# Forgetting attention: next head's first two units scored beside the last unit, with one score buffer that swaps sides per head

## The reference

```python
q = q.reshape(b, lp, B_HEADS, HEAD_DIM)          # 8 heads of 64; k and v alike
cum = jnp.swapaxes(jnp.cumsum(log_f, axis=1), 1, 2)
for i in range(lp // Q_BLOCK):                    # 128 queries at a time
    lo, hi = i * Q_BLOCK, (i + 1) * Q_BLOCK
    s = jnp.einsum('bqhd,bkhd->bhqk', q[:, lo:hi], k[:, :hi]) * (HEAD_DIM ** -0.5)
    s = s + cum[:, :, lo:hi, None] - cum[:, :, None, :hi]
    mask = (idx[None, :hi] <= idx[lo:hi, None]) & key_valid[None, :hi]
    p = jax.nn.softmax(jnp.where(mask, s, -jnp.inf), axis=-1)
    outs.append(jnp.einsum('bhqk,bkhd->bqhd', p, v[:, :hi]))
```

## Time and profile before

| what | us |
|---|---|
| median of the runs | 2371.5 |
| profiled execution, its own time | 2372.46 |
| span of its trace | 2370.8 |
| forgetting attention, from first to last transposes | about 503 (648 to 1151) |
| TensorE busy, whole span | 2140.1 (90%) |
| VectorE busy, whole span | 1652.2 (70%) |
| ScalarE busy, whole span | 1484.8 (63%) |

### The profile page before, as it was taken

One profiled execution on the slowest core, in us unless ns is written; L12 is line 12 of the kernel. 1 busy time (PEld: TensorE's weight loads), 2 busy tenths in 40 slices (PEclk: granted clock), 3 DMA queues, 4 the chain that ended last, 5 costly groups with the idle time before them and its releaser, 6 DMA issues. The chain is left out here.

```text
span 2370.8 us, 35822 instructions
## 1 busy us (share of the span) xinstructions
PE 2140.1 (90%) x11168; PEld 1772.0 (75%) x11168; DVE 1652.2 (70%) x3067; ACT 1484.8 (63%) x2262; POOL 487.2 (21%) x561
## 2 busy tenths in 40 slices
PE   6999999779699999999799975999999999999980
PEld 6798989656477777777688864878888888888860
DVE  5323232367588888888533347989999999999976
ACT  5323241286587787777533322878888888788867
POOL 0112111153123323221000001122222222222221
PEclk9999999889899999999899986999999999999995
DMA  6536352633442222222233325997877869999838
GB/s 205 183 111 195 118 186 86 177 70 97 112 121 66 59 61 55 66 64 87 81 124 142 142 98 208 365 347 240 285 258 248 282 214 362 321 311 298 265 86 301
DMA packets 220553, 420.60 MB, mean 177 GB/s; under 512 B 47912, under 2 KB 97144, under 8 KB 219288
## 3 DMA queue, kind: packets, MB, share of 16 engines
q1 hardware_dynamic: 187760, 316.08, 39.6%
q0 software_dynamic: 31648, 101.89, 14.9%
q10 hardware_dynamic: 1040, 1.31, 0.2%
HBM read 437.68 MB, written 86.39 MB: 221 GB/s over the span
## 5 line engine op out<-in xcount | busy, mean ns | idle before, releaser
L2539 DVE TENSOR_TENSOR moe_w_lo<-fetch_w_raw,moe_w_hi 128x1024 fp32r<-128x1024 f32 x376 | 435.4, 1217 | 12.5 <-ACT moe_w_hi L2468 12.3
L2468 ACT ACTIVATE moe_w_hi<-fetch_w_raw 128x1024 fp32r<-128x1024 f32 x376 | 369.0, 1053 | 69.1 <-DMA fetch_w_raw<-in_w_e_up_dram 37.1
L2593 PE MATMUL moe_ps_gu<-moe_w_hi,moe_xT_hi 128*128 128x512 f32 x736 | 292.8, 398 | 4.5 <-DVE moe_xT_lo L2550 4.5
L2595 PE MATMUL moe_ps_gu<-moe_w_hi,moe_xT_lo 128*128 128x512 f32 x736 | 288.8, 392 | 0.0
L2594 PE MATMUL moe_ps_gu<-moe_w_lo,moe_xT_hi 128*128 128x512 f32 x736 | 288.5, 392 | 0.0
L1571 DVE TENSOR_TENSOR fox_p_lo<-fox_ps_t,fox_p_hi 128x512 fp32r<-128x512 f32 (+4 forms) x352 | 211.4, 612 | 46.6 <-ACT fox_p_hi L1504 44.8
L1504 ACT ACTIVATE fox_p_hi<-fox_ps_t 128x512 fp32r<-128x512 f32 (+4 forms) x352 | 182.0, 533 | 84.9 <-PE fox_ps_t L1642 84.0
L2545 DVE TENSOR_TENSOR moe_d_lo<-fetch_d_raw,moe_d_hi 128x1024 fp32r<-128x1024 f32 x184 | 213.1, 1220 | 10.8 <-ACT moe_d_hi L2476 8.5
L1642 PE MATMUL fox_ps_t<-ident,fox_s 128*128 128x128 f32 (+1 forms) x1216 | 197.6, 277 | 22.2 <-ACT fox_s L1497 22.0
L1558 DVE CUSTOM_DVE_ANT_0 fox_s<-fox_ps_r,fox_ncum 128x512 f32<-128x512 f32 (+4 forms) x352 | 191.2, 569 | 17.2 <-PE fox_ps_r L1627 10.0
L1497 ACT ACTIVATE fox_s<-fox_s,fox_ntop 128x144 f32<-128x144 f32 (+5 forms) x192 | 173.6, 906 | 27.0 <-DVE fox_ntop L1566 27.0
(11 more groups left out here) (346 smaller groups left out, 5136.8 us busy)
## 6 DMA issues: line engine op xcount, KB each, us to landing
fetch_w_raw<-in_w_e_gate_dram SPq DMA_DIRECT2D x192, 512.0 KB
fetch_w_raw<-in_w_e_up_dram SPq DMA_DIRECT2D x192, 512.0 KB
fetch_d_raw<-in_w_e_down_dram SPq DMA_DIRECT2D x92, 1024.0 KB
ahead_raw<-in_w_in_dram SPq DMA_DIRECT2D x24, 1024.0 KB, 5.2
gates_wide<-in_x_dram SPq DMA_DIRECT2D x16, 512.0 KB
h<-gates_wide POOLq DMA_DIRECT2D x16, 512.0 KB, 3.3
gates_wide<-qT SPq DMA_DIRECT2D x32, 256.0 KB, 4.4
mix_h<-h SPq DMA_DIRECT2D x16, 512.0 KB, 3.6
```

The lines of the kernel that those rows point to most:

```text
L2468: nc.scalar.activation(w_hi[:, k], w_raw[:, k].rearrange("p j n -> p (j n)"), ACT.Copy).then_inc(gu_high, 1)
L2539: nc.vector.tensor_tensor(w_lo[:, k], w_raw[:, k].rearrange("p j n -> p (j n)"), w_hi[:, k].bitcast(F32), ALU.subtract).then_inc(gu_split, 1)
L2593: nc.tensor.matmul(out, xT_hi[:, slot, k], w_hi[:, k, cols], start=k == 0, stop=False)
L2595: done = nc.tensor.matmul(out, xT_lo[:, slot, k], w_hi[:, k, cols], start=False, stop=k == KT - 1)
```

## The change

The rows of unit n+1 no longer always stand beside the blocks of unit n. Beside g3 of a head now come the 14 rows of g0 and g1 of the next head. Beside g0 (of heads 1 to 7) come the three rows of g2's first tile, beside g1 the other ten rows of g2, and beside g2 the 17 rows of g3, as before. Head 0 keeps the old order up to its g2, and beside the last unit there are no rows, as before. Every instruction is still issued, with the same shapes.

The score buffer becomes one tensor of 12944 columns, with two halves of 5440 (the size of g2) and a tail for the last tile of g3. Even heads keep g0 and g1 side by side in the first half (4736 columns), g2 in the second, and g3 in the first half and the tail; odd heads have the halves the other way round. What VectorE's first write of a unit waits for (`turned_before_rows`) follows from that: g0 and g1 wait until g2 of the head before is turned, g2 until g3 of the head before is, g3 until g1 of its own head is. `ntop` gets a place for each g.

```diff
-        row_at = [[sum(P * (4 * g + i + 1) + META for i in range(j)) for j in range(5)] for g in range(GROUPS4)]
+        SIZES = [[P * (4 * g + j + 1) + META for j in range(4)] for g in range(GROUPS4)]
+        HALF = sum(SIZES[2])
+        S_COLS = 2 * HALF + SIZES[3][3]
+        row_at = []
+        for odd in range(2):
+            near, far = (HALF, 0) if odd else (0, HALF)
+            starts = [near, near + sum(SIZES[0]), far, near]
+            row_at.append([[starts[g] + sum(SIZES[g][0:j]) for j in range(4)] for g in range(GROUPS4)])
+        row_at[0][3][3] = 2 * HALF
...
-        s = [m.sb(f"s{i}", [P, row_at[GROUPS4 - 2 + i][4]]) for i in range(2)]
+        s = m.sb("s", [P, S_COLS])
-        ntop = m.sb("ntop", [P, 2, 4])
+        ntop = m.sb("ntop", [P, GROUPS4, 4])
...
+        def rows_during(n):
+
+            if n < 0:
+                return range(rows_before[0], rows_before[1])
+            h, g = units[n]
+            if g == GROUPS4 - 1:
+                return range(rows_before[n + 1], rows_before[n + 3]) if h + 1 < B_HEADS else range(0)
+            if h > 0 and g < 2:
+                first, last = rows_before[n + 2 - g], rows_before[n + 3 - g]
+                cut = first + sum(1 for r in range(first, last) if rows[r][1] == 0)
+                return range(first, cut) if g == 0 else range(cut, last)
+            return range(rows_before[n + 1], rows_before[n + 2])
+
+        def turned_before_rows(n):
+
+            h, g = units[n]
+            if g == 3:
+                return blocks_before[n - 1]
+            if h == 0:
+                return 0
+            return blocks_before[n - g] if g == 2 else blocks_before[n - g - 1]
...
-                if n + 1 < UNITS:
-                    g = units[n + 1][1]
-                    ahead = range(rows_before[n + 1], rows_before[n + 2])
-                    rate = SPREAD / len(ahead)
-                    events += [(rate * (i + 0.5), "scores", r) for i, r in enumerate(ahead)]
-                    for j in range(4):
-                        done = sum(len(row_chunks(4 * g + i)) for i in range(j + 1))
-                        events.append((rate * (done + 0.4), "tops", 4 * (n + 1) + j))
-                        mine = [r for r in range(pieces_before[n + 1], pieces_before[n + 2]) if pieces[r][1] == j]
-                        events += [(rate * (done + 0.8) + 0.14 * SPREAD * (i + 0.5) / len(mine), "exp", r)
-                                   for i, r in enumerate(mine)]
+                ahead = rows_during(n)
+                rate = SPREAD / max(1, len(ahead))
+                events += [(rate * (i + 0.5), "scores", r) for i, r in enumerate(ahead)]
+                for i, r in enumerate(ahead):
+                    unit, j = rows[r][0:2]
+                    if r + 1 < len(rows) and rows[r + 1][0:2] == (unit, j):
+                        continue
+                    events.append((rate * (i + 1.4), "tops", 4 * unit + j))
+                    mine = [p for p in range(pieces_before[unit], pieces_before[unit + 1]) if pieces[p][1] == j]
+                    events += [(rate * (i + 1.8) + 0.14 * SPREAD * (c + 0.5) / len(mine), "exp", p)
+                               for c, p in enumerate(mine)]
...
-                    if n >= 2:
-                        dve.wait_ge(p_turned, blocks_before[n - 1])
+                    wait(dve, p_turned, turned_before_rows(n))
...
```

More of the change, by code:

```diff
@@ L1491, in exponential @@
                 n, j, c, key, width = pieces[r]
-                g = units[n][1]
+                h, g = units[n]
                 act.wait_ge(maxed, 4 * n + j + 1)
                 wait(act, summed, n - GROUPS4 + 1)
-                at = row_at[g][j] + key
-                here = s[g % 2][:, at:at + width]
-                nc.scalar.activation(here, here, ACT.Exp, bias=ntop[:, n % 2, j:j + 1],
+                at = row_at[h % 2][g][j] + key
+                here = s[:, at:at + width]
+                nc.scalar.activation(here, here, ACT.Exp, bias=ntop[:, g, j:j + 1],
                                      accum_out=part[g][:, j, c:c + 1]).then_inc(probs, 1)
@@ L1553, in maxima @@
                         dve.wait_ge(cum_in[h % 2], 16 * (h // 2 + 1))
-                    if n >= 2:
-                        dve.wait_ge(p_turned, blocks_before[n - 1])
+                    wait(dve, p_turned, turned_before_rows(n))
                 dve.wait_ge(rows_done, r + 1)
-                at = row_at[g][j] + key
-                nc.vector.tensor_tensor_reduce(out=s[g % 2][:, at:at + width], in0=ps_r[ring_of["row", r] % R_BANKS][:, 0:width],
+                at = row_at[h % 2][g][j] + key
+                nc.vector.tensor_tensor_reduce(out=s[:, at:at + width], in0=ps_r[ring_of["row", r] % R_BANKS][:, 0:width],
                                                in1=ncum[:, h % 2, key:key + width], scale=1.0, scalar=10 * MASK,
@@ L1565, in tops @@
                 dve.wait_ge(biased, rows_before[n] + sum(len(row_chunks(4 * g + i)) for i in range(j + 1)))
-                nc.vector.tensor_reduce(ntop[:, n % 2, j:j + 1], mx[g][:, j], AX.X, ALU.max, negate=True).then_inc(maxed, 1)
+                nc.vector.tensor_reduce(ntop[:, g, j:j + 1], mx[g][:, j], AX.X, ALU.max, negate=True).then_inc(maxed, 1)
             def probabilities_low(k):
@@ L1640, in turn @@
                         pe.wait_ge(probs, pieces_before[n] + sum(len(row_pieces(4 * g + i)) for i in range(j + 1)))
-                    at = row_at[g][j] + (0 if b == TILES else META + b * P)
-                    done = nc.tensor.transpose(out[0:keys, j * P:(j + 1) * P], s[g % 2][:, at:at + keys], ident[:])
+                    at = row_at[h % 2][g][j] + (0 if b == TILES else META + b * P)
+                    done = nc.tensor.transpose(out[0:keys, j * P:(j + 1) * P], s[:, at:at + keys], ident[:])
                 done.then_inc(p_turned, 1)
```

## The result

The changed kernel takes 2339.9 us (median of four runs, 2339.1 to 2345.0) where the kernel before takes 2371.0 in the same series: 31.1 us less, a ratio of 0.9873 (95% interval 0.986 to 0.9886). The forecast was 2344.5 with a range of 2339 to 2354. So sign and size are right, and the gain is 4 us larger than the 27.0 of the sum.

The account below looks back on a forecast made before the run. The prediction took TensorE as the bound, with holes at unit boundaries and a falling clock. Holes 12.8, less 2.8 for new ones, plus clock 17.0 made 27.0 us off 2371.5: 2344.5 us, range 2339 to 2354.

Parts of the forecast that it names:

- The bound: Forgetting phase: TensorE bounds, busy 478 of 510 us, with some 32 us of holes at unit boundaries, plus its clock loss.
- The clock, 17.0 us: After g1's start in heads 1 to 7: lost full-speed time comes back, four times 1.7 and three times 3.4 us.
- Rival 1: TensorE's clock still falls, after a remaining or new hole: 2361.5 us, chance 0.08.
- The holes, 12.8 - 2.8 = 10.0 us: g1's start, seven heads: holes of 0.18, 1.40 and 0.25 us go, 12.8 us; new small holes take 2.8 back.
- What is late next in g0: Shortened g0: the copy out of `ps_o` and VectorE's low parts come close to late, 0.4 us a head, 2.8 us back.
- The hole at g2's start: The 0.22 us hole there stays, since the last exponential keeps its place: 0, bounds -0.2 and +1.0 us a head.
- Rival 2: The wait only moves to g2's start, hole some 1.5 us and clock falling there: about 2370.5 us, chance 0.05 (together).
- The cause of the 1.40 us hole: At g1's start: VectorE falls behind in g0, needing 6.9 us where TensorE needs 6.62.
- The 3 and 10 split: g2's rows beside g0 and g1: g1 gets 13.6 us on TensorE, g2's start hole stays, 0 gained.
- holes of 0.87 us never brought it down: After g3's start TensorE idles 0.87 us and its clock stays at 1.00 in all eight heads; reason for taking 17.0 us.

Follow-up runs that it names:

- the run with the hole put back: Changed kernel, first turn of g1 in heads 1 to 7 also waiting for two exponentials of g2's first tile: 2366.5 us, ratio 0.998 to before.
- the filled kernel: Kernel before, plus five unneeded 512-column matmuls ahead of the first turn of g1 in heads 1 to 7: 2358.5 us, ratio 0.9941.
- the split of 6 and 7: Changed kernel with g2's rows divided 6 beside g0 and 7 beside g1, instead of 3 and 10: 2374.1 us, ratio 1.002.

## Why the prediction was right, and where it was not

**The bound** was right: TensorE at the unit boundaries and its clock. The layout and the waits on turned blocks cost nothing in the old order, and GpSimd's splits and the loads end none of TensorE's waits in heads 1 to 7 of the changed kernel, as costed. The nine rows stay hidden beside g3, where TensorE remained the bound: 20.23 us busy where 20.9 was forecast, VectorE 17.78 for 18.9, ScalarE 17.33 for at most 18.6. g3 lasts 20.8 us, under the 21.5 to 22 of the forecast.

**The clock, 17.0 us.** Right in kind, a little high: 14.8 us when only the hole's emptiness is removed, at most 16.6 when one is put back. A reason can be that the others catch up while TensorE is slow, so that not all of the slow time is lost; no run tests that by itself. Rival 1 did not come: after the holes that remain, 0.75, 0.22 and 0.57 us in head 3, the clock stays at 1.00.

**The holes, 12.8 - 2.8 = 10.0 us.** Here the sum missed. With the clock's 14.8 apart, the waits brought 31.4 - 14.8 = 16.6 us (16.0 if the clock is taken from the run with the hole put back, 16.6 - 1.2 = 15.4). Three terms were mis-sized.
- *What is late next in g0*, 0.4 us a head: measured 0.00 in g0 and g1 of all seven heads. It should have been at the lower end of its bounds; 2.8 us.
- *The idle column undercounts.* Idle of the whole stretch fell by 11.5 us, but the waits brought 16.6; so 5.1 us of holes were under the modelled ends of TensorE's rows. The 152 turns of head 3 take, from start to start less the idle shown, 14.98 us in the filled kernel and 14.37 in the changed one, at the same clock: 0.6 a head or 4.3 in all. A turn is shown as 0.27 us although the next can follow 0.09 later, so each turn with a hole behind it hides up to 0.18 us. Three such turns a head went, those before the holes of 0.18, 1.40 and 0.25 us. The other 0.8 us is not placed. The Trainium skill, "Perfetto Trace Analysis", section "Tensor Engine Instruction (MATMUL, LD_WEIGHTS)", says that the end of a TensorE instruction is estimated and not observed. The trace agrees, with turns shown as 0.27 us that start 0.09 apart.
- *The hole at g2's start*, costed at 0 with bounds of -0.2 and +1.0: measured +0.53 a head of idle in g2, 3.7 us back, while g3's fell from 0.87 to 0.57, 2.1 us gained (why, no run shows). The prediction kept g2's start as it was since "the last exponential of g2 sits at the same place among g1's blocks"; that step failed, as the top moved behind one block more and so behind a low part. Rival 2's place was real, but not its price; it was a chain on VectorE, not ScalarE's slack.

The first two outweigh the third: 2.8 + 5.1 - 1.6 = 6.3 us more than the 10.0, and the clock 2.2 less, which is the 4 us between 27.0 and 31.1.

**The cause of the 1.40 us hole** was told wrongly. "Behind all is VectorE in g0", meant as a sum of 6.9 us against 6.62, holds for the 0.18 us alone. With VectorE relieved the large hole stayed at 1.37: it is the last tile's chain, in which VectorE counts by what stands ahead of the row and the top, not by its load. The 1.40 went as forecast all the same, because that step rests on the time that the move gives the whole chain, not on VectorE's load. That the row of waits has 2.4 us as its longest, and not 1.4, was misread too (that one is head 0's first turn, which no part of the change touches).

**The 3 and 10 split** was costed at nothing. It is slightly worse than that: 1.4 us of the stretch, in one trace of each kernel.

## What to carry to other kernels

When work in one in-order schedule is spread by shares of a unit's length, a short unit ends before its last chain does; here moving the last tile's chain out of the short unit took the hole away, and moving some of its load did not. A change in the number of rows also shifts every event behind them: look at which side of its neighbours the last top falls, which was worth 0.48 us a head here. In such an order look at what stands ahead of a short instruction that frees a single buffer: here the copy out of `ps_o`, which cost 2.43 and 0.83 us wherever exponentials came before it. And look at a repeated hole on TensorE twice, once for itself and once for the clock after it: the rows of the granted clock say whether it falls there.

## What the runs showed that was not expected

Five matmuls that nobody needs, 1.16 us in each of seven heads, made the kernel 13.5 us faster.

The same hole need not have the same effect on the clock. With the split of 6 and 7 each head's g1 has a hole of 2.43 us and the same 7.57 us of TensorE's work in 10. These are heads 3 and 6:

```profile
845.40:855.40 10.00, 7.57 (x50) 6.08 (x48) 7.28 (x24) 7.20 (x16) 3.91 (x4) 1.00 0.06 16
1031.90:1041.90 10.00, 7.57 (x29) 6.00 (x28) 4.84 (x17) 4.19 (x10) 2.67 (x3) 0.66 0.05 14
```

In heads 2 to 4 the clock stays at 2.4 GHz, in the other four it falls to 1.2. Nor is it the same in each execution: of that kernel's ten, four take 2382.8 to 2383.9 us at a mean clock of 0.949 or 0.950, and six 2366.0 to 2374.9 at 0.952 to 0.956. On the other side, a hole of 0.83 us, with 0.12 of idle close before it, was followed by a fall in three heads of the six that have it. So the prediction's reason "holes of 0.87 us never brought it down" was luck as much as evidence. The Trainium skill, "TensorE: Matmul & The Clock Gate", section "A second HAM failure mode: psum-queue depth-cycling", holds that frequent small idles can make the clock swing; these three heads agree with it, the changed kernel's holes of 0.75 us and less do not. What decides between them stays open.
